# Even mixing phase of a hybrid decoder trunk: delta-rule heads in chunks of 64 tokens, and the output projection's pieces regrouped in the step

## The reference

```
s_kk = einsum('bhvk,bhk->bhv', S, kk_t)
S = S * exp(lw_t) - s_kk * (kk_t * a_t) + v_t * k_t
y_t = einsum('bhvk,bhk->bhv', S, r_t)
...
y = head_groupnorm(y) * ln_w + ln_b + sum(r * k * r_k) * v
o_rwkv = y * silu(gate);   out = concat([o_ret, o_rwkv]) @ w_out
```

## Time and profile before

| | |
|---|---|
| median of 3 runs | 3109.13 us (3108.75 to 3112.86) |
| span of the profiled execution | 3114.7 us |
| busy share of the span | PE 97%, PEld 88%, DVE 60%, ACT 33%, POOL 16% |
| mean granted TensorE clock | 0.982 of full speed |
| even mixing, first matmul to last | 731.2 to 1573 us of the span |

### The profile page before, as it was taken

One profiled execution on the slowest core, in us unless ns is written; L12 is line 12 of the kernel. 1 busy time (PEld: TensorE's weight loads), 2 busy tenths in 40 slices (PEclk: granted clock), 3 DMA queues, 4 the chain that ended last, 5 costly groups with the idle time before them and its releaser, 6 DMA issues. The chain is left out here.

```text
span 3114.7 us, 89589 instructions
## 1 busy us (share of the span) xinstructions
PE 3014.0 (97%) x38876; PEld 2738.6 (88%) x38876; DVE 1862.3 (60%) x3858; ACT 1033.1 (33%) x2337; POOL 504.7 (16%) x519
## 2 busy tenths in 40 slices
PE   9999999996999999999989999999996999999998
PEld 9999999996988888888779999999995788888876
DVE  5311223324777787777445156776665788888876
ACT  4211111113333444343157122222223344444441
POOL 0000000001333333333300000000001111111112
PEclk9999999998999999999899999999998999999999
DMA  4321212215233433333353221221214223333323
GB/s 167 97 74 60 74 61 77 70 47 180 73 102 114 126 120 109 115 125 105 112 184 115 68 70 63 77 77 62 77 47 156 84 84 97 97 97 97 97 96 130
DMA packets 222919, 302.22 MB, mean 97 GB/s; under 512 B 32184, under 2 KB 163520, under 8 KB 222528
## 3 DMA queue, kind: packets, MB, share of 16 engines
q1 hardware_dynamic: 213376, 266.54, 26.4%
q0 software_dynamic: 9152, 29.94, 3.0%
HBM read 200.70 MB, written 95.71 MB: 95 GB/s over the span
## 5 line engine op out<-in xcount | busy, mean ns | idle before, releaser
L363 DVE SCALAR_TENSOR_TENSOR po_stage<-po_work,po_cw,po_stage 128x424 f32<-128x424 f32 (+1 forms) x360 | 232.0, 644 | 27.6 <-issue 0.9
L482 PE MATMUL po_ps<-po_xnT_hi,po_w_hi 128*128 128x424 f32 x960 | 205.0, 355 | 0.0
L482 PE MATMUL po_ps<-po_xnT_hi,po_w_lo 128*128 128x424 f32 x960 | 204.4, 355 | 0.0
L482 PE MATMUL po_ps<-po_xnT_lo,po_w_hi 128*128 128x424 f32 x960 | 204.1, 354 | 0.0
L270 ACT ACTIVATE po_work<-po_ps 128x424 f32<-128x424 f32 (+1 forms) x120 | 61.7, 514 | 408.3 <-PE po_ps L482 408.3
L482 PEld LDWEIGHTS po_ps<-po_xnT_hi,po_w_hi 128*128 128x128 f32 x960 | 180.2, 188 | 5.2
L482 PEld LDWEIGHTS po_ps<-po_xnT_hi,po_w_lo 128*128 128x128 f32 x960 | 180.4, 188 | 4.5
L482 PEld LDWEIGHTS po_ps<-po_xnT_lo,po_w_hi 128*128 128x128 f32 x960 | 180.2, 188 | 4.6
L482 PE MATMUL pe_ps<-pe_w_hi,pe_xnT_hi 128*128 128x256 f32 x1088 | 154.1, 284 | 3.0 <-DVE pe_w_lo L382 2.3
L405 DVE TENSOR_SCALAR pe_stage<-pe_work,pe_cw 128x424 f32<-128x424 f32 (+1 forms) x65 | 28.2, 434 | 208.9 <-ACT pe_work L270 157.8
L482 PE MATMUL pe_ps<-pe_w_hi,pe_xnT_lo 128*128 128x256 f32 x1088 | 152.7, 283 | 0.0
(11 more groups left out here) (463 smaller groups left out, 7237.1 us busy)
## 6 DMA issues: line engine op xcount, KB each, us to landing
me_ring<-scratch_w_lo SPq DMA_DIRECT2D x68, 512.0 KB, 3.8
mo_c<-scratch_ch_o SPq DMA_DIRECT2D x51, 512.0 KB, 3.5
scratch_ch_o<-po_stage SPq DMA_DIRECT2D x96, 212.0 KB, 1.9
scratch_tok_e<-pe_stage SPq DMA_DIRECT2D x136, 128.0 KB, 1.9
pe_raw<-in_w_in_e POOLq DMA_DIRECT2D x52, 256.0 KB, 3.8
me_xs<-scratch_ch_e SPq DMA_DIRECT2D x17, 768.0 KB, 6.3
po_raw<-in_w_in_o POOLq DMA_DIRECT2D x48, 256.0 KB, 3.8
scratch_ch_e<-pe_stage SPq DMA_DIRECT2D x52, 212.0 KB, 1.9
```

The source lines that it names most:

```text
L363: return nc.vector.scalar_tensor_tensor(out=o, in0=a, scalar=s, in1=b, op0=op0, op1=op1)
L482: last = nc.tensor.matmul(out, left.bitcast(F32R), right.bitcast(F32R), start=(i == 0 and k == 0), stop=(i == 2 and k == KD - 1))
```

## The change

The delta-rule heads work in two chunks of 64 tokens for each tile of 128 (`CK = 64`).

- The system is of size 64 in each chunk. Level 64 goes, with `TB` and `low_block`. `TF`, `IL`, `MG` and `G2T` hold two chunks of 64 by 64 instead of one block of 128 by 128.
- The decays are taken from the middle of each chunk (`emid`, `eend`, `fac` get a column per chunk), and the running sum restarts at each chunk.
- The score products become `with_own_chunk`: for each pair of heads and chunk one matmul with 64 stationary columns. `key_side` makes the key and receptance scores of `BK[:, 1]` at once; `key_scores`, which was there already, now makes those of `BK[:, 0]` for both sides, so that `receptance_scores` goes and `low_products` writes `G2T` too.
- The state is advanced twice in a step: `from_state(t, c)`, `solve(t, c)`, `solved(t, c)`, `state_of_chunk(t, c)`, `new_state(t, c)` for c = 0 and 1. The value products of both chunks and of both sides come first of all in the step (`values_part`), with the wait for `mixT_written0` ahead of them. Outputs are made once (`outputs_of_solved`), with the two chunks in swapped halves of C_.
- The right side is copied by ACT instead of DVE, and ACT copies the outputs out of C_ (`outputs_of_values`, event `y_copied`); DVE's `centre` reads that copy and stands after `mask(n, 32)`.
- PE's order is new: the projection's pieces stand as 0 and 1, 2 and 3, 4 and 5, then 6, then 7. Nothing stands between `level_T(n, 8)` and `level_X(n, 16)`, nor between `sums(m)` and `turn_sums(m)`.

More of the change, by code:

```diff
@@ L1201, in _ @@
                 if n is not None:
-                    level(n, 64)
                     outputs_of_retention(n)
@@ L1483, in _ @@
                     split_weights(3)
-                if t == 0:
-                    dve.wait_ge(s_wl[7], 16)
-                if t is not None:
-                    solved(t)
+                if t is not None and t < PT:
+                    new_state(t, 0)
                 if n is not None:
@@ L1491, in _ @@
                     keys(m)
-                if t is not None and t < PT:
-                    new_state(t)
                 if n == 0:
@@ L1526, in _ @@
                     mask(n, 32)
+                if t is not None and t < PT:
+                    centre(t)
+                if n is not None:
                     diagonals(n)
@@ L1606, in sample_state_products, with values_part @@
                 sample_ret_state(0, 1)
-            def right_side(t):
+            def values_part(t):
                 if t == PT:
@@ new lines, in values_part @@
+                if t == 0:
+                    await_(pe, "low_read", 1)
+                await_(pe, "mg_read", t)
+                await_(pe, "tok_written", t)
+                for h in range(H):
+                    cols = slice(h * WN, (h + 1) * WN)
+                    for w, bank in enumerate((A_, C_)):
+                        for c in range(2):
+                            at = rows_of(c)
+                            mm(bank[rows_of(c ^ w), cols], MG[at, h, w, :], tokV[t % 2][at, h, :], start=h == 0, stop=t == PT and c == 1 and h == H - 1)
@@ new lines, in solve, with state_of_chunk @@
+            def solve(t, c):
+                at = rows_of(c)
+                if c == 0:
+                    pe.wait_ge(s_ptc, LV[t + 1])
+                    await_(pe, "diagonals_copied", t)
+                    await_(pe, "ret_state_new", min(t, PT - 1))
+                await_chunk(pe, "rhs_copied", t, c)
+                for h in range(H):
+                    last_op = mm(B_[at, h * WN:(h + 1) * WN], TF[at, h, :], rhs[at, h, :])
+                last_op.then_inc(E["u_ready"], 1)
+            def state_of_chunk(t, c):
+                at = rows_of(c)
+                if c == 0:
+                    await_(pe, "mixT_written1", t - 1)
+                for left, right in ((tokK, tokV[t % 2]), (tokB, wv)):
+                    if left is tokB:
+                        await_chunk(pe, "wv_ready", t, c)
+                    for b in range(4):
+                        for half in range(2):
+                            p0 = 64 * half
+                            last_op = mm(D_[p0:p0 + 64, b * WN:(b + 1) * WN], left[t % 2][at, b, p0:p0 + 64], right[at, 2 * b + half, :],
+                                         start=left is tokK and b == 0, stop=left is tokB and b == 3)
+                            if left is tokB and b == 3:
+                                last_op.then_inc(E[f"delta{half}_ready"], 1)
@@ L1905, in _, with beside @@
                 last_step = p == PT
+                def beside(count, *parts):
+                    if p is not None and not last_step:
+                        for part in parts:
+                            project(p, part)
+                    elif p is None and n is not None:
+                        keep_clock(count)
                 if t is not None:
-                    right_side(t)
+                    values_part(t)
+                    from_state(t, 0)
                 if n == 0:
@@ L1957, in _ @@
                 if n is not None:
+                    level_X(n, 8)
+                beside(4, 4, 5)
+                if t is not None and t < PT:
+                    outputs_of_solved(t)
+                    state_of_chunk(t, 1)
+                if n is not None:
+                    key_side(n)
+                    level_T(n, 8)
+                beside(4)
+                if t == PT:
+                    sample_wk_state(0)
+                if n is not None:
                     level_X(n, 16)
-                    receptance_scores(n)
                     turn_q_k(n)
```

456 lines of the change are left out of this document (191 added, 265 removed).

## The result

The changed kernel takes 3217.95 us in the median of 4 runs (3205.42 to 3223.76), the kernel before 3110.99 beside it: 1.0337 times as long, 95% interval [1.0313, 1.0362]. That is 107 us more where 52 were forecast. The direction was right, and the time lies 15 us above the range. The profiled execution took 3217.28 us with a span of 3215.5. The kernel before was run again beside each group of experiments and stood between 3111 and 3123 us, so kernels of different groups are compared by their ratios to it.

A forecast was written before the change was run, and what follows sets the result against it. PE's work bounds the kernel before; after, a ring through PE and DVE of 47.8 us plus 0.8 for the clock, 48.6 a step against 44.6. Over 15 steps 60, less 8 at the ends: 52 slower, 3160, range 3085 to 3203.

The forecast's parts named there:

- The ring: Chain closing a step: PE from `values_part` through `turn_factors`, then mostly DVE to the next `values_part`; 47.8 us against 44.6.
- The wait at the start: PE ahead of `values_part`, waiting for DVE's `mixT_written0`: 3 to 4 us idle in each step.
- the wait at the factors: PE ahead of `turn_factors`, waiting for DVE's `factors`: 1.8 us in each step.
- no idle ahead of `lengths`: DVE reaches `lengths` later than PE's sums, so its former 1.83 us of slack there is gone.
- rival 2: Array tiles don't run four at once in `values_part` and `key_side`: 2.2 us a step, 3193 in all; chance 0.12.
- I take 0.8: Allowance per step for PE's lower granted clock next to its new stalls: 0.8 us.
- the upper bound: Half clock over three quarters of the 10 us of critical PE work next to the stalls: 3 us or so a step.
- rival 3: Clock stays low over most of each step's start and factors: 3 us instead of 0.8, 3193 to 3210; chance 0.12.
- 37.8 of PE's work: PE's own work in one full step after the change, without waits: 37.8 us, a fall of 6.8.
- The ends: Outside the full steps: about 4 us gained in the sample tile's step, about 4 in the filling steps, together 8.
- Rival 1: Queues keep up, only the `mixT_written0` wait is left: 42.0 us a step, 3062 in all; chance 0.15.
- the kernel with no wait: PE never waits in a full step: 37.8 us a step, 3000 in all; chance 0.04.

The follow-up runs named there:

- e1_fill: Changed kernel with 20 calls of no use (40 matmuls, 4.6 us) where PE waits at the start of each full step: 3248.8 us.
- the twins: Two changed kernels with 6 matmuls of no use in each full step's start wait, differing only in matmuls once ahead (52 or 32): 3196.8 and 3235.3 us.
- e4: Changed kernel with value and state products split by side, only the C_ side behind the step's start wait: 3192.9 us.
- e2: Changed kernel with the projection's pieces one by one at X2, T2, X4, T4, X8, T8, T16, X32: 3199.5 us.
- e6: Changed kernel with both the value products split around the start wait and projection pieces moved into the tail: 3168.2 us.
- e5: Changed kernel with projection pieces moved into the tail's waits, value products not split: 3197.3 us.
- e7: Changed kernel with 6 matmuls of no use in each full step's start wait and 52 once ahead of the steps: 3196.8 us.
- e8: Changed kernel with 6 matmuls of no use in each full step's start wait and 32 once ahead of the steps: 3235.3 us.

## Why the prediction missed

**The ring was there, as counted.** From X32 to the next `values_part` it was 17.5 us (1145.12 to 1162.61) for 17.4. The wait at the start was 2.9 in the mean for "3 to 4", released by DVE's rounding rest; the wait at the factors 1.2 a step for 1.8; no idle ahead of `lengths`. The two stretches of PE ahead of it were longer, 24.3 for 22.5 to the end of `key_side` (1110.43 to 1134.69) and 10.4 for 7.9 to the end of `turn_factors`; both hold groups at clock 0.50, the second both pauses of the fence above. Four tiles of 64x64 did run at once, 1.09 for 1.08 (1121.71 to 1122.80 in e1_fill), so rival 2 falls. By the rule of the Trainium skill (TensorEngine Tiling (Array Packing), Gotcha 1: PSUM Pressure) that row tiles can't be in one bank together it would have been 4.3. The trace does not agree.

**The step that failed is the clock's.** "I take 0.8, since the DVE part of the ring doesn't feel it." It was a term of the right kind and mis-sized. The clock stood at 0.50 for 10.7 us a step, and at the twins' 0.4 us that is 4.2, five times the 0.8 and above the 3 that I named as the upper bound. The bound was wrong because I put the low clock only next to the two long waits; the trace has 6.1 us of it around the start alone, and 4.6 more behind pauses and waits later in the step. That the DVE part doesn't feel the clock does not carry 0.8: what is slowed are PE's own groups, 3.82 us for 2.12 at the head of the step shown, and the head lies on the ring. This was rival 3, given 0.12, and the time lies above even its 3210. The Trainium skill (TensorE: Matmul & The Clock Gate, HAM oscillation) has the clock lost again at each burst of matmuls when there is idle time between them. The trace agrees: the clock was low around the start of 14 of the 15 full steps.

**A term was missing.** The pauses inside groups, 1.6 us a step after and 0.3 before; with the stops at the edges of groups 1.9. The sum had no term for them. The idle time of the earlier trace rows was used as an example of the clock, and its cause was not looked for. Timeline of PE before:

```profile
1401.47 0.67 PE L1575 MATMUL me_b<-me_TA,me_ILc 32*32 32x32 f32 x54
1403.88 0.28 PE L1575 MATMUL me_b<-me_TA,me_ILc 32*32 32x32 f32 x10 [1.74 <-issue]
```

It is such a pause, after 54 of 64 matmuls, and ends at such a border.

Put together, a step was forecast as 37.8 of PE's work, 10 of waits, 0.8 of clock, 48.6. Measured it is 42.2 busy, less 4.2 for the clock 38.0; waits 10.0 less 1.6, 8.4; clock 4.2; pauses 1.6: 52.2. So work +0.2, waits -1.6, clock +3.4, pauses +1.6. This sorts PE's time; it does not prove that each microsecond of a term lengthens the ring by as much, since a slower PE also waits less for DVE.

**The ends were wrong in sign.** Over 15 steps the trace has 107 us where 60 were forecast. The sample tile's step gained 5 for 4. The filling steps, forecast to gain 4, lost 12, all of it in the step of t = 0 (41.0 us before, 801.69 to 854.86 after): the reason was not looked for, but taking the wait at the start apart (e4) gave 8 of them back. The odd mixing's 13 us were forecast by nobody; it was luck that they hid part of the miss.

**The pairs had no price in my sum** except X16's copy. By themselves they cost 70 us in the kernel before. In the changed kernel spreading them over eight levels is worth 18. That this is less because other waits there take up the same idle time is a guess, as e2 leaves two of the old places empty.

**Rival 1** (queues keep up) and the kernel with no wait stayed out: even the best arrangement has a step of 46.4, of which idle is 3.6 and PE's work, with what the split adds, 42.8.

What stays open: how much of the time, not of the low clock, belongs to the waits and how much to the pauses. For the low clock both do it: where the wait at the start went and the pauses stayed (e6 for e5) it fell from 9.5 to 3.9; where the wait was half filled in both and only the borders moved (e7 for e8), from 9.0 to 3.2. How the step divides between them was not taken apart. No chunked kernel came below the kernel before.

## What to carry over

When PE goes from never idle to idle in each step, count the granted clock as a term of its own: here every microsecond at 0.50 cost PE 0.4 us of busy time, 4.2 a step, and it was the largest part of the miss. Matmuls of no use in half of such a wait kept the clock up around it (0.5 and 0.7 us at 0.50 for 6.1), but whether they pay in time is not shown: the mean of the twins' ratios is 1.0315, the changed kernel's 1.0337, and the borders decide between the twins. Filling that overruns the wait costs (e1). A run of small matmuls is also a run of instructions: a long piece between them is not only cover for a copy, and a step whose instruction count is near a multiple of 256 has its pauses at the same place each time, good or bad.

## What the hardware showed

Each of the 360 pauses inside groups of small matmuls stands at a 16.4 KB border of PE's instructions, and a packet of the instruction queue started 2.1 to 3.3 us before its end. Moving the borders by 80 instructions, with the same work in each step, changed the time by 38.5 us (1.2%). Not every border pauses. Over the 14 steps of the 16 profiles, of the borders whose 256 instructions took under 3.5 us without the pause, 260 had one of over 0.3 us and 119 had none; of the slower ones 118 had one and 1263 had none. And one side of the value products, on two of four tiles, takes 1.07 us (1102.81 to 1103.88 in e4_split) where both sides together take 1.09.
